# Attention stage: a head's last two value products come before the next head's first two score blocks, and the first row maxima start two units earlier

## The reference

```python
def block(args):
    qn_b, qr_b = args
    s = (jnp.einsum('bqhd,bkhd->bhqk', qn_b, k_nope)
         + jnp.einsum('bqhr,bkr->bhqk', qr_b, k_rope)).astype(jnp.float32)
    p = jax.nn.softmax(s * scale, axis=-1).astype(v.dtype)
    return jnp.einsum('bhqk,bkhd->bqhd', p, v)
```

## Time and profile before

| | us |
|---|---|
| median of 3 runs | 2258.86 (2254.39 to 2260.4) |
| the profiled execution, its own time | 2260.4 |
| span of that execution in the profile | 2258.6 |
| TensorE busy | 2113.2 (94%) |
| VectorE busy | 952.5 (42%) |
| GpSimd busy | 780.8 (35%) |
| ScalarE busy | 671.7 (30%) |

### The profile page before, as it was taken

One profiled execution on the slowest core, in us unless ns is written; L12 is line 12 of the kernel. 1 busy time (PEld: TensorE's weight loads), 2 busy tenths in 40 slices (PEclk: granted clock), 3 DMA queues, 4 the chain that ended last, 5 costly groups with the idle time before them and its releaser, 6 DMA issues. The chain is left out here.

```text
span 2258.6 us, 28050 instructions
## 1 busy us (share of the span) xinstructions
PE 2113.2 (94%) x11544; PEld 1945.4 (86%) x11544; DVE 952.5 (42%) x1372; ACT 671.7 (30%) x954; POOL 780.8 (35%) x512
## 2 busy tenths in 40 slices
PE   7499999999999988999978799999999999999995
PEld 2479999999999977788868777999999999999994
DVE  2613534444313227555523338342344334433348
ACT  1334232323213242677653211311111121112120
POOL 0324352526112414444432632422332233223234
PEclk9699999999999989999999899999999999999998
DMA  6356211112121256233145432211111111111113
GB/s 235 112 198 97 39 52 32 52 31 66 59 67 49 92 146 185 62 85 84 53 145 163 137 130 75 94 44 41 47 38 47 38 47 43 42 38 47 47 66 130
DMA packets 189103, 183.88 MB, mean 81 GB/s; under 512 B 52743, under 2 KB 156896, under 8 KB 188976
## 3 DMA queue, kind: packets, MB, share of 16 engines
q1 hardware_dynamic: 187680, 177.37, 26.6%
q0 software_dynamic: 1296, 4.72, 0.6%
HBM read 141.32 MB, written 40.74 MB: 81 GB/s over the span
## 5 line engine op out<-in xcount | busy, mean ns | idle before, releaser
L129 POOL TENSOR_TENSOR s_w_lo<-s_w_raw,s_w_hi 128x1024 fp32r<-128x1024 f32 x86 | 219.7, 2555 | 511.4 <-ACT s_w_hi L124 511.4
L821 PE MATMUL s_psum<-h_hi,s_w_hi 128*128 128x384 f32 x1008 | 344.5, 345 | 26.4 <-POOL h_lo L250 26.4
L2465 PE MATMUL s_ps<-h_hi,s_w_hi 128*128 128x384 f32 x1056 | 353.1, 334 | 0.7 <-ACT gate_pad L2309 0.7
L2465 PE MATMUL s_ps<-h_hi,s_w_lo 128*128 128x384 f32 x1056 | 352.9, 334 | 0.0
L2465 PE MATMUL s_ps<-h_lo,s_w_hi 128*128 128x384 f32 x1056 | 352.8, 334 | 0.0
L821 PE MATMUL s_psum<-h_hi,s_w_lo 128*128 128x384 f32 x1008 | 338.1, 338 | 0.0
L821 PE MATMUL s_psum<-h_lo,s_w_hi 128*128 128x384 f32 x1008 | 338.0, 338 | 0.0
L821 PEld LDWEIGHTS s_psum<-h_hi,s_w_hi 128*128 128x128 f32 x1008 | 190.6, 190 | 36.6 <-issue 19.4
L2465 PEld LDWEIGHTS s_ps<-h_hi,s_w_hi 128*128 128x128 f32 x1056 | 198.2, 188 | 1.4 <-issue 1.0
L2465 PEld LDWEIGHTS s_ps<-h_lo,s_w_hi 128*128 128x128 f32 x1056 | 198.2, 188 | 0.4
L2465 PEld LDWEIGHTS s_ps<-h_hi,s_w_lo 128*128 128x128 f32 x1056 | 198.2, 188 | 0.0
(11 more groups left out here) (362 smaller groups left out, 3849.0 us busy)
## 6 DMA issues: line engine op xcount, KB each, us to landing
s_w_raw<-in_w_ffn_in SPq DMA_DIRECT2D x44, 512.0 KB, 3.7
s_w_raw<-in_w_in SPq DMA_DIRECT2D x41, 512.0 KB, 3.9
s_w_mod<-in_w_mod SPq DMA_DIRECT2D x8, 2048.0 KB, 8.1
w_raw<-in_w_ffn_out SPq DMA_DIRECT2D x11, 1024.0 KB, 4.9
scratch_gates<-sig SPq DMA_DIRECT2D x48, 192.0 KB, 1.9
merge_gates<-scratch_gates SPq DMA_DIRECT2D x16, 576.0 KB, 3.8
w_mod<-in_w_mod SPq DMA_DIRECT2D x4, 2048.0 KB, 10.4
scratch_o_mla<-o_raw SPq DMA_DIRECT2D x8, 576.0 KB, 4.7
```

The costliest lines, as they stand in the source:

```text
L129: pool.tensor_tensor(flat[0], flat[1], flat[2], ALU.subtract).then_inc(self.lo_ready, 1)
L821: return pe.matmul(bank(j), wx[c % 2][:, k, :], hx[:, k, j * CH:(j + 1) * CH], start=(k == 0 and n == 0), stop=(k == KD - 1 and n == 2))
L2465: mm = pe.matmul(ps[bank][:, 0:CH], a[s][:, k, :], b[:, k, j * CH:(j + 1) * CH], start=n == 0, stop=n == 3 * KD - 1)
```

## The change

Five edits, all in the attention stage:

- `FIRST_TOPS`: head 0's maxima begin after unit 26 (they began after unit 28), two per unit up to unit 31 and one per unit from unit 32 on. `C` and `T` come after units 38 and 39 (both came after unit 37).
- `H` and `G` of head 0 stand after unit 21 (they stood after unit 24). `H` of head h+1 stands at the start of head h, and no longer at the end of head h-1.
- In `HEAD_ITEMS` `V` u comes before the `M` items that it followed, `C` and `T` come one score block later, and `S` 0 and `S` 1 of the next head come after `V` 8 and `V` 9.
- `V` 9 sums in the second half of `ps_s1` and no longer in `ps_m0`. Its wait for `C` goes, and so does the wait of `M` 0 for the copy to `o_raw`; `S` 1 of a later head gets a wait for that copy. The rings of `p_hi` and `p_lo` restart with each head.
- ScalarE's second half of the rotary weight split (six short copies, L1757 and L1758) stands before unit 13 instead of unit 19; GpSimd's wait for the second half of `uq_lo` at unit 16 goes.

```diff
@@ -1370,16 +1370,17 @@
-    FIRST_TOPS.setdefault(B_UNITS[B_AT["q", 3, 0] + _n // 2], []).append(_n)
+    FIRST_TOPS.setdefault(B_UNITS[B_AT["q", 2, 0] + 4 + (_n // 2 if _n < 12 else _n - 6)], []).append(_n)
 HEAD_ITEMS = (
-    ("L", 0), ("S", 2), ("L", 1), ("M", 0), ("M", 1), ("V", 0), ("M", 2), ("M", 3),
...
-    ("S", 9), ("Dk", 0), ("H", 0), ("L", 8), ("V", 7), ("S", 10), ("L", 9), ("V", 8), ("V", 9), ("S", 11), ("Dv", 0))
+    ("L", 0), ("H", 0), ("S", 2), ("L", 1), ("V", 0), ("M", 0), ("M", 1),
...
+    ("S", 8), ("L", 7), ("T", 0), ("V", 6),
+    ("S", 9), ("Dk", 0), ("L", 8), ("V", 7), ("L", 9), ("V", 8), ("V", 9), ("Dv", 0),
+    ("S", 10), ("S", 11))
@@ -1510,7 +1511,7 @@
-        ps_oc = ps_m[0][:, 0:TC]
+        ps_oc = ps_s[1][:, 1, 0:TC]
@@ -1552,7 +1553,7 @@
-                if (kind, x, u) == ("q", 2, 2):
+                if (kind, x, u) == ("q", 1, 2):
                     item("H", 0, 0)
                     item("G", 0, 0)
@@ -1563,13 +1564,12 @@
             item("Dv", 0, 1)
-            item("H", 0, 1)
             for h in range(HEADS):
                 for kind, u in HEAD_ITEMS:
-                    if kind[0] in "DH":
+                    if kind[0] == "D":
                         if h < HEADS - 2:
                             item(kind, u, h + 2)
-                    elif kind in "GMPCT":
+                    elif kind in "HGMPCT":
                         if h < HEADS - 1:
                             item(kind, u, h + 1)
@@ -1688,8 +1688,6 @@
                             pe.wait_ge(k_loaded[e], 32 * (h // 2 + 1))
-                            if h >= 2:
-                                pe.wait_ge(o_read, 2 * (h - 1))
@@ -1698,6 +1696,8 @@
+                        if u == 1 and h > 0:
+                            pe.wait_ge(o_read, 2 * h)
@@ -1720,18 +1720,13 @@
-                        if u == 9:
-                            if h < HEADS - 1:
-                                pe.wait_ge(top.taken, top.at[h + 1, "C", 0] + 1)
-                            else:
-                                pe.wait_ge(o_read, 2 * h)
...
-                                last = pe.matmul(ps_oc, a[e][:, 9, :], x[(10 * h + 9) % P_RING][:, 0:TC], start=(m == 0), stop=(m == 2))
+                                last = pe.matmul(ps_oc, a[e][:, 9, :], x[9 % P_RING][:, 0:TC], start=(m == 0), stop=(m == 2))
@@ -1767,7 +1762,7 @@
-                    if n == 19:
+                    if n == 13:
                         split_uq_rot(1)
@@ -1889,9 +1884,7 @@
-                        if (x, u) == (0, 0):
-                            pool.wait_ge(uq_lo_ready, 2)
-                        if (x, u) == (3, 0):
+                        if (x, u) == (2, 0):
                             pool.wait_ge(q_lo_ready, 1)
@@ -1900,11 +1893,11 @@
                         if h == 0:
-                            pool.wait_ge(q_roped, 9)
+                            pool.wait_ge(q_roped, 6)
```

More of the change, by code:

```diff
@@ L1730, in item @@
                             if u == 9:
-                                last = pe.matmul(ps_oc, a[e][:, 9, :], x[(10 * h + 9) % P_RING][:, 0:TC], start=(m == 0), stop=(m == 2))
+                                last = pe.matmul(ps_oc, a[e][:, 9, :], x[9 % P_RING][:, 0:TC], start=(m == 0), stop=(m == 2))
                             else:
                                 for j in range(2):
-                                    last = pe.matmul(ps_o[:, j, :], a[e][:, u, :], x[(10 * h + u) % P_RING][:, j * 512:(j + 1) * 512],
+                                    last = pe.matmul(ps_o[:, j, :], a[e][:, u, :], x[u % P_RING][:, j * 512:(j + 1) * 512],
                                                      start=(u == 0 and m == 0), stop=(u == 8 and m == 2))
@@ L1817, in item @@
                         act.wait_ge(exp_done, 10 * h + u + 1)
-                        act.activation(p_hi[(10 * h + u) % P_RING][:, 0:width], prob[u % 2][:, 0:width], ACT.Copy).then_inc(hi_ready, 1)
+                        act.activation(p_hi[u % P_RING][:, 0:width], prob[u % 2][:, 0:width], ACT.Copy).then_inc(hi_ready, 1)
                     if kind == "V" and u >= 8:
@@ L1867, in item @@
                         dve.wait_ge(hi_ready, 10 * h + u + 1)
-                        dve.tensor_tensor(p_lo[(10 * h + u) % P_RING][:, 0:width], prob[u % 2][:, 0:width], p_hi[(10 * h + u) % P_RING][:, 0:width],
+                        dve.tensor_tensor(p_lo[u % P_RING][:, 0:width], prob[u % 2][:, 0:width], p_hi[u % P_RING][:, 0:width],
                                           ALU.subtract).then_inc(lo_dve, 1)
@@ L1906, in item @@
                         pool.wait_ge(hi_ready, 10 * h + u + 1)
-                        pool.tensor_tensor(p_lo[(10 * h + u) % P_RING][:, :], prob[u % 2][:, :], p_hi[(10 * h + u) % P_RING][:, :],
+                        pool.tensor_tensor(p_lo[u % P_RING][:, :], prob[u % 2][:, :], p_hi[u % P_RING][:, :],
                                            ALU.subtract).then_inc(lo_pool, 1)
```

## The result

| | before | after |
|---|---|---|
| median of 4 runs each, us | 2256.62 (2253.55 to 2260.4) | 2271.59 (2267.34 to 2272.81) |
| profiled execution, own time / span | 2260.4 / 2258.6 | 2273.02 / 2271.2 |
| TensorE busy | 2113.2 | 2119.6 |

The ratio is 1.0062, 95% interval 1.004 to 1.0085: slower by 9 to 19 us. Forecast: 2272.0, range 2262 to 2281. The medians differ by 15.0 us, where 13.3 was forecast. That the time itself came within 0.4 us of 2272 is in part luck: the forecast started from a median of 2258.86, and with one more run the median of before is 2256.62.

The account below looks back on a forecast made before the run. TensorE, busy 30.00 of 30.00 us in full heads, was taken as the bound, so reordering there only opens gaps. 15.7 + 0.1 - 2.5 = +13.3 us gave 2273.7 profiled, 2272 as median; range 2262 to 2281.

Parts of the forecast that it names:

- `V` 8, seven times 1.1: At seven ends of heads TensorE waits 1.1 us before `V` 8 for `L` 8, 7.7 us in all.
- `V` 0, seven times 0.8: At seven ends of heads TensorE waits 0.8 us before `V` 0 for the chain behind `S` 0, 5.6 us in all.
- `M` 0, six times 0.4: In heads 1 to 6 TensorE waits 0.4 us before `M` 0 for `H`, 2.4 us in all.
- The sum of the three: The gaps before `V` 8, `V` 0 and `M` 0 together: 15.7 us, bounds 6.7 and 18.3.
- The new wait of `S` 1 at nothing: At ends of heads, `S` 1's wait for the copy to `o_raw` costs nothing, at most 0.2 us.
- The row of maxima adds nothing: At ends of heads the maxima row returns from memory before `S` 0, due 5.97 us after `T`; nothing added.
- First part +0.1: Before head 0: `S` 0 starts at 903.4 against 903.29, +0.1 us, bounds -3 and +2.
- First head -2.5: In the first head `V` 0 fills the hole before `M` 0: gain 2.5 us, 3.0 at full clock, 1.4 if it falls.
- Its low sum, 6.7 + 0.1 - 1.4: Low end of the forecast's own range, 2265: lower gap bounds, first part +0.1, first head's gain 1.4 us.
- The clock did not fall at the ends of heads: Rival: short stops at ends of heads lower the clock, 1.7 us lost each, 12 in all, 2284 us; chance 0.12.
- The gaps were not hidden: Rival: gaps at ends of heads mostly hidden, 0.36 + 0.8 remain per head, about +6, 2265 us; chance 0.11.
- too small to turn the sign: Rival: faster, about 2256 us, with -3 in the first part and -3.0 in the first head; chance 0.07.

Follow-up runs that it names:

- e3: The changed kernel with `T` put back by one score block, between `V` 5 and `S` 8; 2268.90 us, ratio 1.0049 to the kernel before.
- e4: The changed kernel with `H` put back behind `S` 9, two heads ahead; 2269.44 us, ratio 1.0058 to the kernel before.
- e9: The changed kernel with `S` 0 back between `V` 7 and `V` 8, `H` behind `S` 9 and `T` before `S` 8; 2274.49 us, ratio 1.0081.
- e5: The changed kernel with `S` 0 back between `V` 7 and `V` 8 and rings running on over heads; 2303.22 us, ratio 1.0202.
- e14: The kernel before with only ScalarE's constant rows moved from among the v units to after unit 21; 2256.82 us, ratio 0.9994.
- e12: e9 with `V` 9 back in `ps_m0` and the old waits of `V` 9 and `M` 0; 2252.83 us, ratio 0.9977 to the kernel before.
- e13: The heads of e12 on the old first part, with ScalarE's constant rows moved to after unit 21; 2253.73 us, ratio 0.9979.
- e11: The heads of e9 on the old first part, with ScalarE's constant rows moved to after unit 21; 2273.65 us, ratio 1.0073.

## Why the prediction was right

*`V` 8, seven times 1.1.* Measured 1.15, by the chain as worked out (`L` 8 3.00 after `S` 8, `V` 8 at 4.27 against 4.28). Of the 1.15, 0.1 is the slower restart. e3 shows both causes: `T` (4.0 / 7 = 0.57) and the missing `S` 0.

*`V` 0, seven times 0.8.* Measured 0.86. The chain from the end of `S` 0 needed 3.63, as forecast.

*`M` 0, six times 0.4.* Measured 0.40 and 0.1 behind it; e4 takes the wait away. The sum of the three was 15.7 and came out 16.85. The restarts, which the prediction did not count, have the size of the difference: 0.1 seven times in `V` 8 and six times behind `M` 0, 1.3 us.

*The new wait of `S` 1 at nothing.* Right for this order. e9 shows that it is the order that makes it free.

*The row of maxima adds nothing.* Right in the trace of after, where no `S` 0 waits for it, but by a margin of 0.1 us that was not seen: e5's row needed 3.74 from `mx_hi`, and the change gives it 3.83. The row was later than that now and then (4.4 and 4.5 us in e9, 5.15 in e14), so some luck is in it. The prediction took the distance from `T` (5.97), which held since `mx_hi` comes 2.22 after `T` in both orders. The Trainium skill, "DMA: Bandwidth & Descriptors", section "Anatomy of one DMA — SWDGE (gpsimd) path", gives about 2.0 us of fixed cost for one DMA issued through GpSimd, so for two in a row some 4 us, as an estimate. The trace does not agree for these two, which SyncE issues: in e5 it was 936.56 less 933.45 (`mx_lo`'s end), 3.1.

*First part +0.1.* Measured -0.13, with parts that were wrong and cancel, and within the scatter of this part (2 us): that the number is so close is luck. The six copies did delay the store of head 0's q, by 0.86 us (39.70 us after the stage's first matmul against 38.84), but the load of `qf` behind it was issued 0.05 us earlier; what took up the delay in between is not shown. So `M` 0 was 0.09 later, not 1.1, and TensorE's stop was 3.52 us, not 4.7. VectorE began at 863.62 (864.04 on the scale of before) and not 865.4. Behind it the prediction let an idle time of 0.80 us on VectorE go. It grew to 2.19 instead: `M` 2 waited 2.08 us for the reduction (1.73 in the same place before), and behind the longer stop the clock was low for longer (0.50 and 0.68 over 864 to 872, where before had 0.95 and 0.63), which the prediction had only as a bound. So `T` still came at 891.55 (891.97 on the scale of before, forecast 892.2).

*First head -2.5.* Measured -2.92. The clock stayed up, which the prediction had at less than certain, and rightly: in three of the eleven traces with `V` 0 first it fell.

*The range.* Its low sum, 6.7 + 0.1 - 1.4, takes the first part at its middle and the first head at its dearest. With the lower bounds that the prediction gives for both (-3 and -3.0) it is +0.7, about 2260. The measured loss is far from either.

*The rivals.* The clock did not fall at the ends of heads. It did in e9, behind a single longer wait. (The row that the prediction names for this rival, 903.3 to 912, has 1.00; the fall is in the window behind it.) The gaps were not hidden, and the first head's gain (2.9 us) was too small to turn the sign.

## What to carry to other kernels

Before an item is moved behind another, take the chain on the other engines from the end of what feeds it (here 3.63 us for exponential, hi part and lo part) and compare it with TensorE's own work in between; the difference is paid at each end of a head. Items hang together: the places of `S` 0 and `T` and the bank of `V` 9 cost no wait in heads 1 to 6 of the old set, and where only some of them were put back it cost 18 us (e9) and 45 us (e5) against the kernel before, more than the 15 us of the whole change. A gap of the first head alone (2 to 3 us, once) is won without any of this, by `V` 0 ahead of `M` 0 (e12, e13).

## What the runs showed of the hardware

Two kernels left TensorE idle for about the same time in the heads. These are their whole heads parts, after and then e9:

```profile
902.74:1162.96 260.22, 245.92 (x1094) 193.72 (x1094) 125.32 (x187) 171.56 (x191) 114.96 (x48) 1.00 0.25 62
```

```profile
902.91:1167.62 264.71, 249.70 (x1094) 201.66 (x1094) 125.31 (x187) 171.96 (x191) 114.93 (x48) 0.97 0.22 61
```

In after 14.3 us are idle, cut into stops of 0.9 us and less from head 1 on, and the granted clock stayed at 1.00. In e9 15.0 us are idle, with one stop of 1.7 us a head, and the clock was at 0.97 in the mean, so part of the time at 1.2 GHz. It fell behind five of the seven stops of e9, and behind six of the seven of e11, which has the same heads: a stop of this length doesn't bring it down each time. e9's heads are 20.7 us longer than e12's. Its rows show 12.7 us of waits that e12 hasn't (11.9 for `o_raw`, 0.8 for the row of maxima), and the clock took some 8 us (0.03 of 264.71), against some 2 in e12; together that is most of it.

The Trainium skill, "TensorE: Matmul & The Clock Gate", section "A second HAM failure mode: psum-queue depth-cycling", speaks of short idle times between groups of matmuls that make the clock go back and forth. e9 shows such a case, the changed kernel one in which it doesn't happen. What in the stops decides was not tried by itself.
